# A one-layer retention and state-space step on eight cores: the first projections read x·(1+scale) alone, loads in a new order, state outputs in tile layout, exponent matmuls over 24 rows

## The reference, cut to what matters

```python
h = x * (1 + sc1) + sh1                 # sc1, sh1, g1, sh2, sc2, g2 = silu(cond) @ w_ada + b_ada
proj = h @ w_in                          # q k v g | z | x B C | dt
# group A, retention: 4 heads of 128, both directions, rotary on latent tokens
o_ret = silu(g) * rms_norm(bidir_scan(q, k, v, v, lg_f, lg_b, s0_f, s0_b))
# group B, SSD: 8 heads of 64, 2 B/C groups, state 128
xbc = silu(depthwise_conv(xbc, conv_w, conv_b))     # 5 taps, zero padding at both ends
y = bidir_scan(cm, bm, xs * dt_f, xs * dt_b, la_f, la_b, s0_f, s0_b) + d_skip * xs
o_ssd = rms_norm(y * silu(z)) * ssd_norm_w
x = layer_norm(ALPHA * x + g1 * (concat(o_ret, o_ssd) @ w_out), ln1_g, ln1_b)
h2 = x * (1 + sc2) + sh2
x = layer_norm(ALPHA * x + g2 * ((silu(h2 @ w_gate) * (h2 @ w_up)) @ w_down), ln2_g, ln2_b)
# outputs: x of context and latent tokens, and the context's final scan states (ret and ssd)
```

## Time and profile before

| | us |
|---|---|
| median of 3 runs, slowest core | 763.19 (762.35 to 763.46) |
| profiled execution, span of its slowest core, core 2 | 765.7 |
| spans of the eight cores | 747.8 to 765.7 |
| PE busy on core 2 | 682.8 (89%) |
| DVE, POOL, ACT busy | 400.0, 308.4, 297.7 |
| chain that ended last | PE 75%, DMA 16%, DVE 3% |

### The profile page before, as it was taken

The page is one execution under the profiler, slowest core; times in us unless marked ns, Lnnn a source line. Parts: engine busy times, 40 slices in busy tenths (PEclk is TensorE's granted clock), DMA queues, the critical chain, the costliest instruction groups (busy, mean ns, idle before and its releaser), DMA issues.

```text
span 765.7 us, 13115 instructions; the slowest of 8 cores (747.8 to 765.7 us)
## 1 busy us (share of the span) xinstructions
PE 682.8 (89%) x4261; PEld 356.3 (47%) x4336; DVE 400.0 (52%) x830; ACT 297.7 (39%) x470; POOL 308.4 (40%) x351
## 2 busy tenths in 40 slices
PE   0449999799998979998996999999999999999994
PEld 0226565455665545554443544444444444444441
DVE  4564567338986898886585321221212122376545
ACT  2668565366676546443545311111111110032222
POOL 7330234179724724554115699100000000088764
PEclk9969899899999999999996999999999999999997
DMA  8997379970267932326035032222664503012112
GB/s 258 338 302 178 55 125 150 164 130 16 57 134 158 165 98 56 56 63 130 19 124 135 7 76 47 45 50 55 131 131 110 131 1 76 0 56 83 56 55 83
DMA packets 19618, 78.51 MB, mean 103 GB/s; under 512 B 5968, under 2 KB 8272, under 8 KB 12512
## 3 DMA queue, kind: packets, MB, share of 16 engines
q0 software_dynamic: 5328, 39.34, 28.8%
q1 hardware_dynamic: 14224, 38.34, 15.6%
HBM read 108.61 MB, written 8.40 MB: 153 GB/s over the span
## 4 chain that ended last, share of the span: by engine, by line
PE 75%; DMA 16%; DVE 3%; issue 3%; SPq 2%; ACT 1%; POOL 1%; DVEq 0%; POOLq 0%; ACTq 0%
PE psum L614 74%; DMA arena<-w_in 6%; DMA arena<-w_gu 4%; DMA ossd<-arena 2%; SPq L185 2%; DVE arena L662 2%; DMA arena<-w_out 1%; DMA arena<-w_ada 1%; PE psum L617 1%; POOL arena L662 1%; ACT arena L639 1%; DVE arena L676 1%; DMA arena<-x 1%; ACT L639 0%; POOL arena L687 0%
## 5 line engine op out<-in xcount | busy, mean ns | idle before, releaser
L614 PE MATMUL psum<-arena 128*128 128x512 bf16 (+8 forms) x4153 | 670.5, 318 | 69.1 <-ACT arena L639 26.1
L614 PEld LDWEIGHTS psum<-arena 128*128 128x128 bf16 (+2 forms) x4228 | 343.7, 100 | 391.9 <-issue 102.5
L662 POOL TENSOR_TENSOR arena<-arena 128x512 f32<-128x512 f32 (+5 forms) x204 | 248.5, 1239 | 193.5 <-ACT arena L639 54.7
L639 ACT ACTIVATE arena<-psum 128x512 bf16<-128x512 f32 (+2 forms) x189 | 105.9, 575 | 265.5 <-PE psum L614 251.2
L662 DVE TENSOR_TENSOR arena<-arena,psum 128x512 bf16<-128x512 bf16 (+2 forms) x124 | 82.6, 675 | 183.8 <-PE psum L614 167.5
L662 DVE TENSOR_TENSOR arena<-psum,arena 128x512 f32<-128x512 f32 (+4 forms) x208 | 127.7, 635 | 70.4 <-PE psum L614 57.9
L639 ACT ACTIVATE arena<-arena 128x512 bf16<-128x512 f32 (+7 forms) x137 | 100.1, 751 | 155.1 <-DVE arena L676 120.2
L676 DVE SCALAR_TENSOR_TENSOR arena<-arena 128x1 f32<-128x1 f32 (+2 forms) x108 | 63.4, 595 | 14.6 <-POOL arena L662 8.1
L639 ACT ACT_TABLE_LOAD x42 | 53.9, 1283 | 29.5 <-PE psum L614 21.4
L185 POOL DMA_DIRECT2D arena<-w_gu x11 | 6.2, 568 | 109.9 <-PE psum L614 104.1
L639 ACT ACTIVATE arena<-psum,arena 128x512 bf16<-128x512 f32 (+3 forms) x66 | 39.8, 632 | 12.8 <-PE psum L614 5.9
(11 more groups left out here) (18 smaller groups left out, 47.2 us busy)
## 6 DMA issues: line engine op xcount, KB each, us to landing
arena<-w_gu POOLq DMA_DIRECT2D x11, 1024.0 KB, 8.6
arena<-w_in POOLq DMA_DIRECT2D x10, 1024.0 KB, 10.8
arena<-w_ada SPq DMA_DIRECT2D x8, 1024.0 KB, 20.5
arena<-w_ada POOLq DMA_DIRECT2D x8, 1024.0 KB, 11.8
arena<-xT SPq DMA_DIRECT2D x6, 1024.0 KB, 23.7
arena<-x SPq DMA_DIRECT2D x12, 512.0 KB, 4.1
arena<-w_down POOLq DMA_DIRECT2D x4, 1408.0 KB, 12.8
y<-arena SPq DMA_DIRECT2D x11, 512.0 KB, 2.6
```

The costliest lines, as they stand in the source:

```text
L614: return P.add({PE: (c, lambda e: e.matmul(R(out), lhsT=R(lhsT), rhs=R(rhs), start=start, stop=stop))}, [lhsT, rhs], [out])
L639: fn = lambda e: e.activation(out=R(out), in_=R(in_), func=func, **{k: R(v) for k, v in kw.items()})
L662: fn = lambda e: e.tensor_tensor(out=R(out), in0=R(in0), in1=R(in1), op=op)
```

## The change

- **Start.** The projections with `w_in0` and `w_in1` read `hA = x*(1+scale)`, which needs w_ada slabs 2 and 3 only. What the shift adds to a projected channel is the same for all tokens of a group; it is computed by 64 small matmuls (`sh1b` with the slabs) and goes into the bias of the convolution (`cvb`, shift times the sum of the taps). The borders of `xbc`, which must stand for zero, are set to minus that amount (`nbsh`). The full `hT` is formed as well, later, for all the other projections.
- **Loads.** SP issues w_ada 2 and 3, then cst, xT of chunk 2 and `w_in0`, smalls, xT of chunk 0, `w_in1` as float32 halves, xT of chunk 1. The shift's slabs 0 and 1 come on POOL, after xT of chunk 0 and after `w_in1`.
- **Exponents.** The split parts are laid out as four groups of 24 rows at partitions 0, 32, 64 and 96, in a left (`rsL`) and a right (`rsR`) array. For each tile one product with a mask (`rb`) is made on DVE or POOL, and each E is one matmul over 24 rows with 512 columns. `cstb` and its load are gone.
- **State outputs** are written as [4, 128, 512] and [2, 2, 128, 512]; the host rearranges them.
- **Late part.** `wo_load` and GA's out stage come after GB's heads, gated by `hb[3]`, at level 1.5. `x1` goes to DRAM after its affine part and is read back before `down`.
- **Planner.** `place` tries more orders; where the arena is too small, `schedule` runs again under a cap on live bytes.

```diff
-EARLY_B, EARLY_CK = True, (2, 0)
     ada_f32(2)
-    ada_f32(0)
+    ada_f32(3)
+    P.dma(SP, cst, cf_d[:, 0:396])
     xT_load(2, 0)
     half_load("w_in0", w0, w_in_d[0], 0)
-    P.dma(SP, smalls, brow(R_SMALL, 48))
-    if EARLY_B:
-        xT_load(0, 0)
-    ada_f32(3)
-    ada_f32(1)
     xT_load(2, 1)
     o_w0 = half_load("w_in0", w0, w_in_d[0], 1)
+    P.dma(SP, smalls, brow(R_SMALL, 48))
+    xT_load(0, 0)
     xT_load(0, 1)
-    w_in[1] = slab_load("w_in1", w_in_d[1], 4096, after=[o_w0])
+    half_load("w_in1", w1, w_in_d[1], 0)
+    o_w1 = half_load("w_in1", w1, w_in_d[1], 1)
+    xT_load(1, 0)
+    xT_load(1, 1)
+    ada[0] = slab_load("ada0", w_ada_d[0], 4096, after=[xTo[(0, 1)]])
+    ada[1] = slab_load("ada1", w_ada_d[1], 4096, after=[o_w1])
...
+            scaled(hA3[ck][:, kt, :], xT[(ck, q)][:, (kt % 4) * 512:(kt % 4) * 512 + 512], sc1p[q][:, kt % 4, c:c + 1])
...
+            for kt in range(8):
+                mm(ps[:, j * 2:j * 2 + 2], wv[:, kt, j * 128:(j + 1) * 128], sh1b3[:, kt, :], kt == 0, kt == 7)
...
+        ts(nbsh3[:, sl, :], p3, -1.0, ALU.mult)
+        tt(bsh3[:, sl, :], p3, sumw[:, sl].unsqueeze(2).to_broadcast([128, 4, 2]), ALU.mult)
...
-                act(dst[:, o + s:o + s + w], ps, AF.Silu, bias=cols[:, C_CONVB + ct:C_CONVB + ct + 1])
+                act(dst[:, o + s:o + s + w], ps, AF.Silu, bias=cvb3[:, ct, g:g + 1])
...
-                    early = i == 0 and ck in EARLY_CK
-                    ps, o = fm(w, j, ck, pool="start" if early else "dense", early=early)
+                    early = i == 0 and ck == 2
+                    ps, o = fm(w, j, ck, pool="dense" if ck == 1 else "start", early=early, h=hA3)
...
+        tt(rb.rearrange("p (a t) -> p a t", a=4), rsR[g][:, tok].unsqueeze(1).to_broadcast([128, 4, 128]),
+           blkm.unsqueeze(2).to_broadcast([128, 4, 128]), ALU.mult, (DVE, POOL))
...
-                mm(E[d], r96, selbias[0:96, d, gg * 512:(gg + 1) * 512], True, False)
-                for h in range(4):
-                    mm(E[d][:, h * 128:h * 128 + 128], selrow[0:96, d * 8 + gg * 4 + h, :], r96, False, h == 3)
+                r0 = (d * 2 + gg) * 32
+                mm(E[d], rsL[g][r0:r0 + 24, tok], rb[r0:r0 + 24, :], True, True)
...
-            P.dma(SP, ossd_d[(t0 - 8) // 2, 1].rearrange("h n e -> n h e"), v8(S), is_out=True)
+            P.dma(SP, ossd_d[(t0 - 8) // 2, 1], S, is_out=True)
...
-            P.dma(SP, oret_d[:, :, h].rearrange("s d p e -> p s d e"), stS.rearrange("p (s d e) -> p s d e", s=2, d=2), is_out=True)
+            P.dma(SP, oret_d[h], stS, is_out=True)
...
+            x1r = rx1()
+            P.dma(SP, x1r, x1_d[t * 128:(t + 1) * 128, :], after=[x1w[t], fmm[8]])
+            norm(u, banks, x1r, gate)
...
-    oA = out_stage(GA, "dense", 1.2, [last_h[1]])
...
+    wo_load(0)
+    wo_load(1)
+    oA = out_stage(GA, "dense", LV_B, [hb[3]])
     oB = out_stage(GB, "mix", LV_B, [hb[4]])
...
+            x1w[t] = P.dma(SP, x1_d[t * 128:(t + 1) * 128, :], x1[t])
```

More of the change, by code:

```diff
@@ L24 @@
     __slots__ = ("idx", "eng", "alts", "is_dma", "nbytes", "deps", "inc", "cval", "fin", "npend", "succ", "start", "key",
-                 "allocs", "touch", "sem", "is_out", "table", "tag", "cost", "ready", "done", "fn", "w", "pal")
+                 "allocs", "touch", "sem", "is_out", "table", "tag", "cost", "ready", "done", "fn", "w", "pal", "forced")
     def __init__(self, idx, alts, key, tag):
@@ L209, in whole, with schedule @@
                         o.deps |= {d for d in q.deps if d.idx < o.idx or (mms and d not in s)}
-    def schedule(self, extra):
+    def schedule(self, extra, cap=None):
         ops = self.ops
+        sbt, sleft, mlive, mpark = {}, {}, [0], []
+        if cap is not None:
+            for b in self.bufs:
+                sleft[b] = len(b.ops)
+                for o in b.ops:
+                    sbt.setdefault(o.idx, []).append(b)
+        seen = set()
         for o in ops:
-            o.succ, o.done, o.w = [], False, []
+            o.succ, o.done, o.w, o.forced = [], False, [], False
         for o in ops:
@@ L317, in schedule @@
                     best = cand
+            if best is None and mpark:
+                x = min(mpark, key=lambda o: o.key)
+                mpark.remove(x)
+                x.forced = True
+                push(x, x.ready)
+                continue
             if best is None:
@@ L340, in schedule @@
             st = max(t, o.ready)
+            grow = sum(b.nbytes for b in sbt.get(o.idx, ()) if b not in seen)
+            if grow and mlive[0] + grow > cap and not o.forced:
+                mpark.append(o)
+                continue
             if o.allocs:
@@ L361, in schedule @@
             o.eng, o.fn, o.cost, o.start, o.done = e, fn, cost, st, True
+            freed = False
+            for b in sbt.get(o.idx, ()):
+                if b not in seen:
+                    seen.add(b)
+                    mlive[0] += b.nbytes
+                sleft[b] -= 1
+                if sleft[b] == 0:
+                    mlive[0] -= b.nbytes
+                    freed = True
+            if freed and mpark:
+                mp, mpark[:] = list(mpark), []
+                for x in mp:
+                    push(x, max(x.ready, o.start + cost))
             tcur[e] = st + cost
@@ L398, in place @@
             live.append((t0, t1, b))
[L399 to L413 removed]
+        n = len(live)
@@ new lines, in place, with fit @@
+        t0s, t1s = np.array([x[0] for x in live]), np.array([x[1] for x in live])
+        size = np.array([float(x[2].nbytes) for x in live])
+        meet = (t0s[:, None] < t1s[None, :] + slack) & (t0s[None, :] < t1s[:, None] + slack)
+        self.peak = max(float(size[(t0s <= t) & (t1s >= t)].sum()) for t in t0s)
+        self.top = self.peak
+        if self.peak > ARENA:
+            return None
+        def fit(order):
+            off, end, put = np.zeros(n), np.zeros(n), np.zeros(n, bool)
+            for i in order:
+                m = meet[i] & put
+                cur = 0.0
+                if m.any():
+                    o = off[m]
+                    s_ = np.argsort(o)
+                    st = np.concatenate(([0.0], np.maximum.accumulate(end[m][s_])))
+                    gap = np.concatenate((o[s_], [1e12])) - st
+                    cur = st[np.argmax(gap >= size[i])]
+                off[i], end[i], put[i] = cur, cur + size[i], True
+            return end.max(), off, end
@@ new lines, in place @@
+        rng = np.random.RandomState(7)
+        best = None
+        for key in (lambda x: (x[2].nbytes < 4096, x[0]), lambda x: (-x[2].nbytes * (x[1] - x[0] + 20), x[0]),
+                    lambda x: (-x[2].nbytes, x[0]), lambda x: (-x[2].nbytes, x[0] - x[1])):
+            kept = cur = sorted(range(n), key=lambda i: key(live[i]))
+            top = None
+            for it in range(tries):
+                got = fit(cur)
+                if top is None or got[0] <= top:
+                    top, kept, res = got[0], cur, got
+                if top <= ARENA:
+                    break
+                pos = {i: float(j) for j, i in enumerate(kept)}
+                for i in np.nonzero(res[2] > top - 1)[0]:
+                    pos[i] = rng.uniform(-1, pos[i])
+                for i in rng.randint(0, n, 4):
+                    pos[i] = rng.uniform(-1, n)
+                cur = sorted(kept, key=lambda i: pos[i])
@@ L414, in place @@
             if best is None or top < best[0]:
-                best = (top, placed)
+                best = (top, [(live[i][0], live[i][1], live[i][2], int(res[1][i])) for i in range(n)])
+            if top <= ARENA:
+                break
         self.top = best[0]
         if self.top > ARENA:
-            pts = sorted(set(x[0] for x in live))
-            self.peak = max((sum(x[2].nbytes for x in live if x[0] <= t <= x[1]), t) for t in pts)
             return None
```

184 lines of the change are left out of this document (97 added, 87 removed).

## The result

The changed kernel is slower: 777.4 and 785.4 us in two runs, against 763.5 us (762.4 to 765.2) for the kernel before. The ratio is 1.022, interval 1.016 to 1.029. The forecast was 736.6. The profiled execution of the changed kernel took 777.4 us, its slowest core, core 7, spans 776.1; what follows is read from that core.

What follows compares the result with a forecast made beforehand. PE was taken to set the pace except at the start, a few middle stops, the hand-over and the tail. Terms -6.5 + 1 - 11.1 - 2 - 8 + 0 = -26.6 gave 736.6 us from the median, range 723 to 756.

Steps and rivals of the forecast that it cites:

- 8.5 us ahead: Start: by 64 us PE would have done 26.8 us of full-speed work instead of 18.3; net -6.5 after 64 new matmuls.
- I take +1: Start: second set of 24 affine pieces, 6.6 us on each of two engines, costs +1 us, bounds 0 and +4.
- 60 to 70 open matmuls: Start: when the shift arrives at 63.4 us, 60 to 70 projection matmuls (13 to 15 us) are still open.
- -5.5: Start: -6.5 us net from earlier projections, with +1 for the second set of affine pieces.
- The exponents, -11.1: Exponent tables: 48 tables each fall from 0.45 us to one 0.219 us step, -11.1 us, bounds -11.1 and 0.
- The forecast's own sign: Exponent tables: the prediction is wrong if steps around the 24-row matmuls are longer than 0.3 us.
- at most 1.07 once: Exponents: the rb products on POOL are ready tiles ahead and cost 0, or at most 1.07 us once if late.
- The stores, -2: State outputs: 2 KB rows in place of 256-byte pieces shorten the ossd wait, -2 us, bounds 0 and -6.
- The hand-over, -8: Stop at 403 to 417: matmuls kept back cover the 12.9 us wait for w_gu, -8 us, bounds 0 and -11.
- heads without that filler, 0: GB's heads, 237 to 353: without GA's out stage, PE and DVE lose about equal shares, 0, bounds -5 and +8.
- x1 through DRAM, 0: Late part: twelve stores and twelve loads of 512 KB fit where DMA is 27% busy, 0 us.
- (c): Rival, slower: shift's slabs wait for arena room, stalling all behind hT; slower past 107 us, 768 at 112; chance 0.07.

Runs made afterwards that it cites:

- e2: Kernel before with new planner, tile-layout state outputs and GA's out stage (with w_out loads) behind GB's heads; old start and exponents: 745.9 us, ratio 0.975 to before.
- e15: e8 with four rb buffers in place of two: 751.8 us, ratio 0.980 to the kernel before.
- e7: e2 plus the change's new start with its own load order, old exponents: 776.0 and 779.3 us in two runs.
- e6: e2 plus the new start, with the shift's slabs moved to SP as float32 halves right behind w_in0: 761.3 us, ratio 0.990 to the kernel before.
- e11: e2 with the load of w_dt moved behind that of the rope tables: 755.9 us, ratio 0.982 to the kernel before.
- e18: The whole change with four rb buffers in place of two: 784.8 us, ratio 1.020 to the kernel before.
- e13: e9 with four rb buffers in place of two: 752.3 us, ratio 0.980 to the kernel before.
- e16: e12 run again, on the same chip as e14: 742.8 us, ratio 0.969 to the kernel before.
- e17: Kernel before with the tile-layout state outputs alone, planned by the change's planner: 763.0 us, ratio 0.992 to the kernel before.
- e8: e2 plus the 24-row exponents and x1 through DRAM, old start: 769.9 us, ratio 1.000 to the kernel before.
- e1: The change with each exponent table over rows 0 to 95 and rb's mask zero, so exponents are left out: 773.2 and 775.5 us in two runs.
- e3: Kernel before with new planner, tile-layout state outputs and the 24-row exponents alone: 773.7 us, ratio 1.011 to the kernel before.
- e4: Kernel before with new planner, tile-layout state outputs and the new start alone: 805.6 to 817.4 us, most cores at a lower clock.
- e9: e2 plus the 24-row exponents, without the x1 copy: 763.8 us, ratio 0.996 to the kernel before.
- e10: e9 with tables over all 128 rows, using four left factors each masked to one group: 756.7 us, ratio 0.983 to the kernel before.
- e14: e10 with four rb buffers and x1 through DRAM: 753.1 us, ratio 0.983 to the kernel before.
- e12: e2 with x1 written to DRAM and read back before the down stage: 743.6 us, ratio 0.965 to the kernel before.

## Why the prediction was wrong

**The step that failed is in the start**, and it has two halves. "I take 26.8: 8.5 us ahead" assumed PE could use whatever had landed. The loads came as forecast (`w_in0` at 32.3 for 31.8, the last xT at 63.5 for 63.4). But PE had 85 wide matmuls done at 65 us, 85 x 0.216 = 18.4 us of work, against 18.3 before: nothing gained of the 8.5, since PE's fixed order waited for xT of chunk 1 while 43 matmuls of `w_in1` (9.3 us) were ready. And "what depends on them are z and the heads, later than the convolution. I take +1" overlooked the dt projection, which reads `hT` as well, and with it `ssd_prep`, the tables and GB's scans. The last dt matmul starts at 108.8 us, before at 70.7, and the tables ran 33 to 38 us later. The shift itself was not "there" at 63.4: its last values came at 81.5, behind its matmuls in PE's order. The forecast had PE's cover in view (60 to 70 open matmuls when the shift comes), and PE was indeed full from 65 to 127. The bill came 200 us later: scans and heads then fell together in a stretch where DVE sets the pace at 63.0 of 68 us, with few dense matmuls left to fill PE. Against e2, PE idles 12.0 us there instead of 1.4, and about 11 us more go to the lower clock (an estimate: half of the 22.1 us that it works from 280.9 to 308.2): 22 of the 28 us between the two profiled cores (776.1 and 747.8). That it is the dense matmuls used up early that are missing there is inferred from e2, where PE is full beside a DVE just as busy; no run gave them back alone. In numbers, the start costs 30 us over e2 and 30 to 33 over e15, where -5.5 was forecast. Of the 30, some 15 belong to the place of the shift's slabs (e7 against e6, with the reserve on the arena below). Of the other 15, 5 to 10 are those of a late dt projection (e11, whose first dt matmul starts at 91.1 us, like e6's at 90.2). The rest, the second set of affine pieces and the 64 small matmuls, was not run by itself.

**The kernel's own plan** had the sign. By the planner's costs, which are in the source, the plan of the kernel before ends at 734.6 us and that of the change at 738.2; e2 ends at 728.1 and e7 at 743.6, e15 at 727.3 and e18 at 744.3, so that the start costs 15 to 17 us there, half of what was measured. These costs are rough and know no clock, but the forecast summed what the plan had already put in order.

**The exponents, -11.1**, were wrong in sign. A table took 0.44 us of PE before and takes 0.41 now where it stands alone among wide matmuls (0.311 + 0.317 - 0.216), so that PE wins 1.3 us and not 11.1. The drains, 48 x 0.2 = 9.6 us, take back nearly all of it: the 24-row matmul's step was within the stated bound (-11.1 to 0), and the choice of its far end the mistake. The forecast's own sign, steps longer than 0.3 us, came true. By the Trainium skill, page "TensorEngine Tiling (Array Packing)", section "Key Properties", changing the mode drains the engine; this case's trace agrees, with 0.311 and 0.317 for 0.216. By the Trainium skill, page "TensorE: Matmul & The Clock Gate", section "The mechanism", matmuls in different row groups overlap; the trace agrees as well, 3 ns between starts, but the tables hardly ever stand side by side. All told the exponents cost e2 16 us, which the sum did not have: `rb` was costed "at most 1.07 once" by POOL's free time, while its ring of two also ties the order of the tables. e13 takes back 11 of the 16; the medians leave 6 (e13 over e2) to 9 (e15 over e16).

**The stores, -2**: -6 (e17). **The hand-over, -8**: e2 against e17 is 0.975 to 0.992, -13 us. Mechanism and sign were right: `w_gu`'s wait is gone and filler is kept; the term "heads without that filler, 0" came out as a gain, PE's 66.6 us of 68 for 62.1. In the change itself none of this is left: the filler kept back is used up where the late scans stall. **x1 through DRAM, 0**: -2 to -3 by the medians, -5 to -8 by the ratios (0.969 and 0.965 for 0.975; the intervals of e16 and e2 overlap a little). One reading of a row was off: the low clock at 27.20 held for six steps, not nine; no term hangs on it.

The parts do not add up on one scale, since each one's price hangs on the others: over e15 the start is 3.9%, over e8 2.3%. Added up, 763 - 6 - 13 - 3 + 16 + 30 = 787 for a measured 777 to 785.

**The rivals.** (c) had the right sign and the place "all behind hT stands still", with its point at 107 us. The shift came earlier than that, at 81.5, and the kernel was slower all the same, because the point was computed from PE's cover alone. Whether the arena has a part in it stays open. The change, e1, e3, e4, e7, e8, e9, e10, e14 and e18 run under a limit of 188,000 to 204,000 bytes, and e6 and e13, faster by 15 and 11 us than their neighbours e7 and e9, under none. The limit couldn't be lifted alone, since the buffers then don't fit, and it changes nothing in the order of e2 (down to 188,000) or of e13 and e15 (at e9's and e8's limits). Under 188,000 bytes e6 gets another order whose plan takes as long (737.5 for 737.8 us); that order was not run.

**The best version** is e12/e16: old start, old exponents, GA's out stage behind GB's heads, tile-layout outputs, x1 through DRAM. 742.8 and 743.6 us, 3.2 to 3.5% under the kernel before and 5 to 6% under the change by the ratios.

## What to carry to other kernels

Doing dense work earlier is no gain if it is the filler of a later stretch that another engine paces: before you move a load, follow every reader of what becomes late (here dt, through `hT`) to the end of its chain, and not only to the next work that PE has in hand. A fixed order turns one late transfer into a stop even when other data are there; where a plan exists, read what it puts behind which load before you count what PE could do. When matmuls get cheaper by using part of the array, count the steps around them, and look for what the new operand's buffers tie together.

## What the runs showed of the hardware

A 24-row matmul among 128-row ones takes 0.311 us in front and 0.317 behind instead of 0.216 each; over 96 rows it takes 0.215 and 0.220 (e1). Tables in other row groups side by side start 3 ns apart. With DVE at 59 to 64 us of 68 in all these kernels, PE's clock in the same stretch ranged from 1.00 (e2, PE busy 66.6 us) over 0.95 (e13, 60.9) to 0.67 (e18, 55.7), but it does not follow from the busy time alone: e7 worked 55.0 us at 0.95. In the change PE idled 3.9 of the 8.9 us before the clock fell; it then stayed at 1.2 GHz for 27.3 us while PE worked 22.1 of them, and in e18 for 37.5 us with 30.0 worked.
